# A tuned decoder layer on one core: two late halves of the modulation land in other raw buffers, and the last is taken after the first Strassen tile's first low weights

## The reference, cut to what matters

```python
mod = (silu(c) @ w_ada + b_ada).reshape(B, 3, 3, D)      # w_ada is 1024 x 9216: the modulation
h = modulate(rms_norm(x, norm_ffn1_g), mod[:, 0, 0], mod[:, 0, 1])
x = x + 0.5 * mod[:, 0, 2] * swiglu(h, ffn1_w_in, ffn1_w_out)
...   # the mixer with mod[:, 1], then the second SwiGLU with mod[:, 2]
def swiglu(h, w_in, w_out):
    g, u = split(h @ w_in, 2)                              # w_in is 1024 x 5632
    return (silu(g) * u) @ w_out                           # w_out is 2816 x 1024
```

## Time and profile before

| what | us |
|---|---|
| three runs | 879.33, 876.66, 875.43 |
| median | 876.66 |
| span of the profiled execution, first to last instruction | 874.8 |
| TensorE matmul busy | 845.0 (97%) |
| VectorE busy | 641.4 (73%) |
| ScalarE busy | 379.8 (43%) |
| GpSimd busy | 50.4 (6%) |
| TensorE waiting on ScalarE's copy to `ev` at L1842 | 4.2 |
| TensorE waiting on VectorE's `sw_lo_a` at L1842 | 3.0 |
| mean granted clock of TensorE | 0.991 |

### The profile page before, as it was taken

One profiled execution on the slowest core, in us unless ns is written; L12 is line 12 of the kernel. 1 busy time (PEld: TensorE's weight loads), 2 busy tenths in 40 slices (PEclk: granted clock), 3 DMA queues, 4 the chain that ended last, 5 costly groups with the idle time before them and its releaser, 6 DMA issues.

```text
span 874.8 us, 14160 instructions
## 1 busy us (share of the span) xinstructions
PE 845.0 (97%) x5767; PEld 755.0 (86%) x5767; DVE 641.4 (73%) x919; ACT 379.8 (43%) x528; POOL 50.4 (6%) x56
## 2 busy tenths in 40 slices
PE   4899989999999999999999999999999999999996
PEld 3678869888999998888887898899988899999886
DVE  4579977776788877858747779988794588885443
ACT  6233325312466653134424256656511356665323
POOL 0000000000001000000350000000000000100000
PEclk9999998999999999999999999999999999999999
DMA  9997565586566665943534422576663566663222
GB/s 276 291 309 235 160 177 155 167 264 173 133 157 157 160 183 178 299 130 97 154 99 125 143 74 73 140 181 173 193 208 98 137 171 159 155 158 104 86 67 96
DMA packets 214797, 142.02 MB, mean 162 GB/s; under 512 B 6232, under 2 KB 193740, under 8 KB 214732
## 3 DMA queue, kind: packets, MB, share of 16 engines
q1 hardware_dynamic: 209780, 132.19, 52.1%
q0 software_dynamic: 4896, 8.92, 6.2%
q10 hardware_dynamic: 56, 0.01, 0.0%
HBM read 130.08 MB, written 2.10 MB: 151 GB/s over the span
## 4 chain that ended last, share of the span: by engine, by line
PE 81%; DVE 9%; DMA 3%; SPq 2%; issue 2%; ACT 1%; DVEq 0%; ACTq 0%
PE ps L1669 13%; PE ps L1671 13%; PE ps L1670 13%; PE ps L1846 12%; PE ps L1842 12%; PE ps L1844 12%; DVE work L1130 2%; DMA ada_first<-in_w_ada_dram 1%; PE ps L1968 1%; PE ps L1969 1%; PE ps L1970 1%; SPq L469 1%; DVE h_lo L1077 1%; DVE xs L1070 1%; DMA sw_raw<-in_ffn_w_in_dram 1%
## 5 line engine op out<-in xcount | busy, mean ns | idle before, releaser
L1842 PE MATMUL ps<-sums_hi,sw_hi 128*128 128x256 f32 x544 | 152.4, 280 | 4.2 <-ACT ev L832 4.2
L1844 PE MATMUL ps<-sums_lo,sw_hi 128*128 128x256 f32 x544 | 152.9, 281 | 0.0
L1669 PE MATMUL ps<-b_hi,sw_hi 128*128 128x512 f32 (+1 forms) x374 | 143.4, 383 | 0.0
L1670 PE MATMUL ps<-b_lo,sw_hi 128*128 128x512 f32 (+1 forms) x374 | 141.5, 378 | 0.0
L800 ACT CAST sw_hi<-sw_raw 128x1024 fp32r<-128x1024 f32 (+2 forms) x102 | 119.8, 1180 | 31.6 <-DVE sw_raw L1251 19.2
L1842 PE MATMUL ps<-h_hi,sw_hi 128*128 128x256 f32 x408 | 114.3, 280 | 3.0 <-DVE sw_lo_a L1264 3.0
L1846 PE MATMUL ps<-sums_hi,sw_lo_a 128*128 128x256 f32 x408 | 115.7, 284 | 0.0
L1844 PE MATMUL ps<-h_lo,sw_hi 128*128 128x256 f32 x408 | 114.6, 281 | 0.0
L1842 PEld LDWEIGHTS ps<-sums_hi,sw_hi 128*128 128x128 f32 x544 | 102.9, 189 | 4.6 <-issue 4.1
L1264 DVE TENSOR_TENSOR sw_lo_a<-sw_raw,sw_hi 128x1024 fp32r<-128x1024 f32 x68 | 98.9, 1455 | 9.9 <-ACT sw_hi L800 7.6
L1844 PEld LDWEIGHTS ps<-sums_lo,sw_hi 128*128 128x128 f32 x544 | 102.7, 189 | 0.0
(11 more groups left out here) (193 smaller groups left out, 1571.8 us busy)
## 6 DMA issues: line engine op xcount, KB each, us to landing
sw_raw<-in_ffn_w_in_dram SPq DMA_DIRECT2D x170, 256.0 KB, 4.2
sw_raw<-in_w_ada_dram SPq DMA_DIRECT2D x15, 1024.0 KB, 5.6
sw_raw<-in_ffn_w_out_dram SPq DMA_DIRECT2D x32, 384.0 KB, 4.5
sw_raw<-in_ffn_w_out_dram SPq DMA_DIRECT2D x32, 320.0 KB, 3.4
w_raw<-in_ffn_w_in_dram SPq DMA_DIRECT2D x19, 512.0 KB, 5.4
ada_raw<-in_w_ada_dram SPq DMA_DIRECT2D x18, 512.0 KB, 5.4
sw_raw<-sw_raw POOLq DMA_DIRECT2D x34, 256.0 KB, 3.3
ada_first<-in_w_ada_dram SPq DMA_DIRECT2D x14, 512.0 KB, 7.3
```

Source lines behind the costliest of these rows:

```text
L1669: nc.tensor.matmul(dst, w_h, a_h, start=start, stop=False)
L1670: nc.tensor.matmul(dst, w_h, a_l, start=False, stop=False)
L1842: nc.tensor.matmul(dst, w_h[:, k, :], src_hi[:, k, :], start=start and k == 0, stop=False, skip_group_check=True)
L1844: nc.tensor.matmul(dst, w_h[:, k, :], src_lo[:, k, :], start=False, stop=False, skip_group_check=True)
```

## The change

Part 8 gets a third raw buffer, `late_raw`, which lies just ahead of `more_raw`, over `b_lo` 7 to 10 and so over the upper four blocks of `xs`. Part 7 goes to `more_raw`. SyncE's order of loads stays 6, 8, 7, but part 8 now waits for the last low part of the Strassen sums (`hsum_lo` at 4), part 7 for part 5, and `load_up(0, 0)` for part 6. VectorE takes part 8 no longer after part 7 behind plain tile 5, but behind `rest_up(0, 0, 1)` of plain tile 6.

```diff
-    ADA_PLAIN = {0: (0,), 1: (1, 2), 2: (3,), 3: (4,), 4: (5, 6), 5: (7, 8)}
-    ADA_IN = ((0, 2, 4, 6, 7, 20, 21, 22, 23), (1, 3, 5, 8))
+    ADA_PLAIN = {0: (0,), 1: (1, 2), 2: (3,), 3: (4,), 4: (5, 6), 5: (7,)}
+    ADA_LATE = 8
+    ADA_IN = ((0, 2, 4, 6, 20, 21, 22, 23), (1, 3, 5, 7), (ADA_LATE,))
...
+    def ada_buffer(part):
+        return next(b for b in range(3) if part in ADA_IN[b])
...
         with ExitStack() as over_a:
+            before_late = sb("before_late", [P, 8 * KA * TH + 2 * GF * T - KA * T], F32, over_a)
+            late_raw = sb("late_raw", [P, 2, KA // 2, UNIT], F32, over_a)
...
             def load_ada(part):
-                b = int(part in ADA_IN[1])
+                b = ada_buffer(part)
                 n = ADA_IN[b].index(part)
+                if part == ADA_LATE:
+                    sp.wait_ge(hsum_lo[0], 4)
                 for s in range(2):
                     if n:
                         sp.wait_ge(ada_link, used(ADA_IN[b][n - 1], (s + 1) * KA // 2))
...
-            sp.wait_ge(ada_link, used(7))
+            sp.wait_ge(ada_link, used(6))
             for n in range(N0[0]):
                 load_up(0, n)
...
                     add_blocks(0, 0)
                     rest_up(0, 0, 0)
                     rest_up(0, 0, 1)
+                    ada_own(ADA_LATE)
                 elif j == PLAIN[0] - 1:
                     rest_up(0, 0, 2)
```

More of the change, by code:

```diff
@@ L126, in build_program @@
     TAKES = ((0, 2), (2, 8), (8, 12), (12, 13), (13, 14))
-    assert sorted(ADA_IN[0] + ADA_IN[1] + tuple(HOSTED[0].values()) + tuple(HOSTED[1].values())) == list(range(2 * UNITS))
+    assert sorted(sum(ADA_IN, ()) + tuple(HOSTED[0].values()) + tuple(HOSTED[1].values())) == list(range(2 * UNITS))
     def used(part, steps=KD // 2):
         return part // 2 * LINKS + part % 2 * (KD // 2) + steps
+    def ada_buffer(part):
+        return next(b for b in range(3) if part in ADA_IN[b])
     def hosted_before(f, i):
@@ L222, in build_program @@
         with ExitStack() as over_a:
+            before_late = sb("before_late", [P, 8 * KA * TH + 2 * GF * T - KA * T], F32, over_a)
+            late_raw = sb("late_raw", [P, 2, KA // 2, UNIT], F32, over_a)
+        with ExitStack() as over_a:
             before_xs = sb("before_xs", [P, 8 * KA * TH + GF * T + (GF - KD) * T], F32, over_a)
@@ L263, in build_program @@
         first_full = [sem(f"first_full{k}") for k in range(KD)]
-        ada_full = [[sem(f"ada_full{b}{s}") for s in range(2)] for b in range(2)]
+        ada_full = [[sem(f"ada_full{b}{s}") for s in range(2)] for b in range(3)]
         mix_full = sem("mix_full")
@@ L461, in load_ada @@
                     k0 = part % 2 * KA + s * KA // 2
-                    sp.dma_start((ada_raw, more_raw)[b][:, s], w_ada_v[:, k0:k0 + KA // 2, ada_cols(part)])\
+                    sp.dma_start((ada_raw, more_raw, late_raw)[b][:, s], w_ada_v[:, k0:k0 + KA // 2, ada_cols(part)])\
                       .then_inc(ada_full[b][s], 16)
@@ L1140, in ada_own @@
             def ada_own(part):
-                b = int(part in ADA_IN[1])
-                count, raw = 16 * (ADA_IN[b].index(part) + 1), (ada_raw, more_raw)[b]
+                b = ada_buffer(part)
+                count, raw = 16 * (ADA_IN[b].index(part) + 1), (ada_raw, more_raw, late_raw)[b]
                 ada_steps(part, lambda q: raw[:, q // 2, q % 2, :], lambda q: (ada_full[b][q // 2], count))
```

## The result

The changed kernel took 872.85 us in the median of five runs (869.78 to 874.86), the kernel before 876.85 us (875.43 to 879.33). The ratio is 0.9947, with a 95% interval of 0.9926 to 0.9968: faster by 0.5%, or 4.0 us. The profiled execution of the changed kernel took 874.86 us, the longest of the five, with a span of 873.1 us and a mean granted clock of 0.988.

A forecast was written before the change was run, and what follows sets the result against it. TensorE, busy 845.0 of 874.8 us, was taken as the bound, losing time at Strassen tile 0; −3.83 (earlier half product 2) and −2.46 (clock) gave −6.3, so 876.66 became 870.4 us, range 868.5 to 873.8.

The forecast's parts named there:

- rival B: Ahead of half product 2, the clock falls all the same, only −3.83 us remain: 872.8 us; chance 0.13.
- an addition that lands after 122 us: Sign of being wrong: tile 0's adding DMA lands after 122 us, where 120.8 was expected.
- a clock of 0.50 after the gap: Sign of being wrong: TensorE at 0.50 after the gap before half product 2; 1.00 was expected from 128 to 138.
- C's mechanism: Tile 0's raw blocks or adding DMA held up, part 8 adding 2.76 us behind low piece 1: 879.4 us; chance 0.04.
- SyncE issues load_up earlier: Waiting for part 6 instead of 7, load_up(0, 0) is issued at 108.12 instead of 114.71, −6.6 us.
- Part 8 and part 7 load early, at no cost: In SyncE's queue, part 8 is issued at 97.7 us, part 7 before 108.12; the 0.20 us wait goes.
- The first wait goes: TensorE's 1.52 us wait before half product 0 vanishes, low piece 0 being over at 121.3, tile 7 at 123.98.
- The adding DMA, term of 5.06 us: Tile 0's adding DMA takes 5.06 us as before, landing at 120.8; fast end 3.3 us, landing at 119.1.
- Part 8 on the path for 2.76 us: On VectorE, all 2.76 us of part 8 lie between low piece 1 and product 7, from 124.1 to 126.9.
- The gap before half product 2, 1.6 us: TensorE idles from 127.0 to 128.6, 1.6 us, and goes on 3.83 us earlier than at 132.44.
- The clock, −2.46 us: After the 1.6 us gap, half products 2 to 4 lose nothing to the clock, −2.46 us more.
- rival D: The third tile's weights, covered by 1.8 us, come late, or SyncE loads no sooner: 875 us; chance 0.08.

The follow-up runs named there:

- e2: Changed kernel, but load_up(0, 0) waits for part 7 again, so only part 8's new place is left; 879.40 us, 1.0037 of the kernel before.
- c0: The changed kernel run again unaltered, on another call's chip; 871.95 us, 0.9941 of the kernel before.
- c2: The changed kernel profiled once more, unaltered; span 870.5 us.
- e6: Changed kernel, but SyncE waits for tile 0's adding DMA before issuing side 1's loads; 871.11 us, 0.9933 of the kernel before.
- e4: Changed kernel plus 24 filler matmuls between half product 1 and the wait for the copy to ev; 871.21 us, 0.9942 of the kernel before.
- e3: Changed kernel, but part 8 stands one step later, between plain product 7 and its low part; 868.47 us, 0.9912 of the kernel before.
- e1: Changed kernel with new buffers and earlier load, but part 8 taken behind part 7 as before the change; 869.73 us, 0.9928 of the kernel before.
- e5: Changed kernel, but part 8 stands ahead of rest_up(0, 0, 1) instead of behind it; 870.30 us, 0.9926 of the kernel before.
- c1: The kernel before the change profiled once more, unaltered; span 874.5 us.

## Why the prediction was right or wrong

The direction and the range held (forecast 870.4, range 868.5 to 873.8, measured 872.85), but the gain was 4.0 us and not 6.3. The measured time lies outside the forecast's own range of 868.5 to 872; it is within the whole range only because rival B was given room. That it falls on rival B's number, 872.8, is luck: B has half product 2 on time and all of the clock lost, and neither was so on average. Two of the signs that I had named for being wrong appeared in the first profile, an addition that lands after 122 us (122.33) and a clock of 0.50 after the gap, and so did the sign of C's mechanism, a gap above 3 us. My line for a gain of 0.5% stood at 872.3: by medians the gain is 0.46%, by the ratio 0.53%, so on which side it fell is not settled. The steps, one by one:

- *SyncE issues load_up earlier.* Right: the first issue comes at 108.97, forecast 108.12, in an execution in which VectorE's plain product 5 already ran 0.85 us later (108.86, before 108.01). e2 shows that the whole gain hangs on this wait.
- *Part 8 and part 7 load early, at no cost.* Right: neither is waited for.
- *The first wait goes.* Right: no idle time before half product 0. I had tile 7 end at 123.98; TensorE reached its end at 123.4, because its matmuls followed each other faster than in the profile that I read.
- *The adding DMA, term of 5.06 us.* Undersized: 5.55 us in the first profile, 6.54 in c0, 5.89 in c2, mean 6.0. The load before it was a little shorter than my 7.37 us, so from the issue of `load_up` to the addition's landing the three profiles took 0.5 to 0.8 us more than the 12.7 us of the kernel before. I named the load of side 1 beside the addition as the reason for 5.06 rather than 3.3, and e6 bears that out; but I took the overlap to be the same as before, and it is not. GpSimd's second addition is issued when side 1's load has landed, and in the nine profiles that show both with that load beside it, the first landed 0.8 to 0.9 us after the second was issued. Three of them:

```profile
126.63 0.87 POOL L612 DMA_DIRECT2D sw_raw<-sw_raw  x1 [3.25 <-DMA sw_raw<-in_ffn_w_in_dram]
121.54 0.87 POOL L622 DMA_DIRECT2D sw_raw<-sw_raw  x1 [3.73 <-DMA sw_raw<-in_ffn_w_in_dram]
121.12 0.87 POOL L622 DMA_DIRECT2D sw_raw<-sw_raw  x1 [4.58 <-DMA sw_raw<-in_ffn_w_in_dram]
```

  These are the kernel before (first addition landed at 127.42), the changed kernel (122.33) and c0 (122.05). So the end of side 1's load and the end of the addition go together. In the changed kernel SyncE has to wait for the end of plain tile 6 on TensorE before it issues that load (1.0 us in the first profile, 2.1 in c0, where TensorE is slower); in the kernel before it did not. The size still varies: in e4, with the same loads, the addition took 5.0 us.
- *Part 8 on the path for 2.76 us.* Right to the hundredth (125.62 to 128.38), and so is 1.74 us from product 7 to half product 2 (128.38 to 130.12). That it could stand elsewhere at less cost, I did not work out; e3 shows it.
- *The gap before half product 2, 1.6 us.* This is the step that failed. It was a small difference of two ends, and both moved: half product 2 came at 130.12, 129.84 and 129.11 instead of 128.6. That is 1.1 us later on average, of which 0.4 us are the later start of the plain tiles and 0.7 us the longer way to the addition's landing. TensorE was through half product 1 at 126.38, 127.18 and 125.50 instead of 127.0. The gap was 3.74, 2.66 and 3.61 us.
- *The clock, −2.46 us.* Wrong as a certain term: rival B, given 0.13, is what happened in one execution in full and in one in part. From half product 2 to the mark the three profiles took 7.05, 4.56 and 6.08 us: a loss of 2.5, none and 1.5 us, on average 1.3.

The two misses add up. Forecast −6.3, half product 2 later by 1.1, clock by 1.3: −3.9. The mean mark of the three profiles of the changed kernel is 135.59, that of the two of the kernel before 139.55: −4.0, which is the measured difference of the medians. An agreement this close is partly luck, since the marks of the three profiles of one kernel spread over 2.8 us.

What I gave for rival D, the third tile's weights, did not occur: the rest behind the mark is 734.3 to 735.9 us in every profile. That a fall of the clock goes with a long gap is shown by the rows (gaps of 0.17 to 2.66 us kept 1.00 in e1, e3, e5, e6 and c0; gaps of 3.61 to 6.62 us were followed by 0.50 in both kernels and e2), and e4 shows that without a gap it stays at 1.00 with the chain unchanged. The length of the gap does not set the cost: after 6.62 us in e2, half product 2 to the mark took 6.06 us, a loss of 1.5 us, and after 3.74 us it took 7.05. What the clock costs in the median of many runs was not separated by e4.

## What to carry to other kernels

When a load is brought forward, the work that was hidden beside it loses its cover: ask where each piece of filler work now stands in the queue, and put it behind the instruction that others wait for, not ahead of it (here 2.8 us of VectorE work moved by one step gave by medians about as much again as the change). Where a term of the sum depends on an idle time that is the difference of two chains, take its scatter from several executions, and let the clock's part enter as a chance and not as a fact. When a DMA inside SBUF sits on a short chain, try issuing a large load whose data are not needed yet behind it: here that brought half product 2 about 2 us forward in the rows, while the gain in the median was not told from none.

## What the runs showed of the hardware

Two things I had not expected. First, the step from matmul to matmul of 512 columns in the plain tiles (up to about 124 us) is a property of the execution: about 0.233 us in the first profile of the kernel before and in c0, 0.229 us in the first profile of the changed kernel, in c1 and c2 and in the other experiments, at a granted clock of 1.00 in all. Over the eight tiles that moves TensorE by about 1 us (tile 7 of the kernel before ended at 123.98 and at 122.90). In the three profiles of the changed kernel it was the one with the slow step, c0, that had the short gap and kept the clock; three profiles do not make that a rule. Why a step differs from one execution to the next stays open. Second, in c2 TensorE restarted at full clock after 3.61 us of idle time and fell to 0.50 only three matmuls later. The Trainium skill ("TensorE: Matmul & The Clock Gate", What's actually happening) says that the monitor runs freely and not in step with the kernel. The rows here agree with it: gaps of 3.61 and 3.74 us cost 1.5 and 2.5 us, and one of 6.62 us cost 1.5 us.
